# Turning the second branch's queries tile by tile between the products of the last projection

## The reference, cut to what matters

```python
def nsa_mixer(q, kv, gates, g_q, g_kc, g_ks, g_kw, pe_cmp, phi_k1, phi_k2, phi_v1, phi_v2):
    q = rms_norm(q.reshape(B, S, KH, G, dh), g_q)          # 8 heads of 64
    k_c, v_c, k_s, v_s, k_w, v_w = ...                     # six slices of kv, 2 heads each
    ...
    kc = rms_norm(compress(k_c, phi_k1, phi_k2), g_kc)     # compress: gelu(blocks @ w1) @ w2
    vc = compress(v_c, phi_v1, phi_v2)
    s_c = jnp.einsum('bsgqd,bcgd->bsgqc', q, kc)           # compressed branch
    ...                                                    # selected branch: q against k_s, v_s
    ...                                                    # window branch: q against k_w, v_w
    o = g[..., 0:1] * o_cmp + g[..., 1:2] * o_slc + g[..., 2:3] * o_win
```

## Time and profile before

| | us |
|---|---|
| median of 3 runs (761.27 to 831.82) | 761.53 |
| the profiled execution's own time | 763.1 |
| its span, first to last instruction | 761.4 |
| PE matmul busy | 752.5 |
| DVE busy | 420.0 |
| ACT busy | 368.8 |
| POOL busy | 137.7 |

### The profile page before, as it was taken

How to read it: one execution, slowest core, us unless ns; L and a number is a source line. 1 busy time by engine, 2 the same in 40 slices (tenths; PEclk the granted TensorE clock), 3 DMA queues, 4 the chain that set the end, 5 groups by cost and what they waited for, 6 DMA issues and landing times.

```text
span 761.4 us, 10546 instructions
## 1 busy us (share of the span) xinstructions
PE 752.5 (99%) x3869; PEld 629.5 (83%) x3869; DVE 420.0 (55%) x842; ACT 368.8 (48%) x719; POOL 137.7 (18%) x163
## 2 busy tenths in 40 slices
PE   9999989999999999999999999999999999999998
PEld 8998877877997788778888888888888888888886
DVE  5478779779986967648555333333334333333333
ACT  7768367756678887663343333333334232323230
POOL 3110336523556453300022000000000000000000
PEclk9999999999999999999999999999999999999999
DMA  9622121101111021113632332323232323232322
GB/s 339 230 79 66 56 74 67 55 28 56 56 56 56 28 84 36 48 56 89 216 91 85 103 111 84 110 84 111 83 111 84 110 84 111 83 111 84 110 84 110
DMA packets 21826, 70.82 MB, mean 93 GB/s; under 512 B 2448, under 2 KB 3600, under 8 KB 21520
## 3 DMA queue, kind: packets, MB, share of 16 engines
q1 hardware_dynamic: 21632, 70.13, 28.5%
q10 hardware_dynamic: 144, 0.03, 0.0%
HBM read 68.05 MB, written 2.10 MB: 92 GB/s over the span
## 4 chain that ended last, share of the span: by engine, by line
PE 93%; DVE 4%; POOL 1%; ACT 1%; issue 1%; POOLq 0%; DVEq 0%
PE psum L1535 26%; PE psum L1537 26%; PE psum L1536 26%; PE psum L1543 5%; PE psum L1718 4%; PE psum L1695 2%; PE psum L1696 2%; POOL nrstd L758 1%; DVE cmp_in L1262 1%; DVE x2T L1517 1%; PE psum L1550 1%; PE psum L1599 1%; ACT q_st L846 0%; PE psum L1690 0%; PE psum L1758 0%
## 5 line engine op out<-in xcount | busy, mean ns | idle before, releaser
L1133 DVE TENSOR_TENSOR w_lo<-stage,w_hi 128x1024 fp32r<-128x1024 f32 (+4 forms) x104 | 113.9, 1099 | 236.1 <-ACT w_hi L846 235.9
L846 ACT ACTIVATE w_hi<-stage 128x1024 fp32r<-128x1024 f32 (+4 forms) x150 | 125.5, 844 | 167.9 <-DMA stage<-in_panels 167.8
L1535 PE MATMUL psum<-hT_hi,w_hi 128*128 128x512 f32 x384 | 155.9, 406 | 0.0
L1537 PE MATMUL psum<-hT_hi,w_lo 128*128 128x512 f32 x384 | 150.1, 391 | 0.0
L1536 PE MATMUL psum<-hT_lo,w_hi 128*128 128x512 f32 x384 | 149.7, 390 | 0.0
L1535 PE MATMUL psum<-a_hi,w_hi 128*128 128x512 f32 x256 | 99.6, 389 | 0.0
L1536 PE MATMUL psum<-a_lo,w_hi 128*128 128x512 f32 x256 | 99.6, 389 | 0.0
L1537 PE MATMUL psum<-a_hi,w_lo 128*128 128x512 f32 x256 | 99.6, 389 | 0.0
L1537 PEld LDWEIGHTS psum<-hT_hi,w_lo 128*128 128x128 f32 x384 | 72.1, 188 | 15.3
L1536 PEld LDWEIGHTS psum<-hT_lo,w_hi 128*128 128x128 f32 x384 | 72.4, 189 | 12.6
L1535 PEld LDWEIGHTS psum<-hT_hi,w_hi 128*128 128x128 f32 x384 | 72.2, 188 | 12.5
(11 more groups left out here) (240 smaller groups left out, 1178.5 us busy)
## 6 DMA issues: line engine op xcount, KB each, us to landing
stage<-in_panels SPq DMA_DIRECT2D x104, 512.0 KB, 3.5
xT_in<-in_xT SPq DMA_DIRECT2D x8, 256.0 KB, 5.3
x_in<-in_x SPq DMA_DIRECT2D x4, 512.0 KB, 7.5
phi<-in_phi SPq DMA_DIRECT2D x2, 1024.0 KB, 6.2
x2T<-in_xT SPq DMA_DIRECT2D x1, 2048.0 KB, 9.9
out_xT<-x2T SPq DMA_DIRECT2D x8, 256.0 KB, 2.0
stage<-in_panels SPq DMA_DIRECT2D x8, 212.0 KB, 5.3
stage<-in_panels SPq DMA_DIRECT2D x4, 408.0 KB, 3.1
```

What stands on the lines that cost most here:

```text
L846: return nc.scalar.activation(dst, src, ACT.Copy, scale=scale)
L1133: tt_op(w_lo[:, p % SLOTS, cols], stage[:, p % SLOTS, cols], w_hi[:, p % SLOTS, cols].bitcast(F32), ALU.subtract)\
L1535: mm(dst, a_h, b_h, start=start, stop=False)
L1537: return mm(dst, a_l, b_h, start=False, stop=stop)
```

## The change

On PE all eight turns were in one place, after panel 1's products of the last projection, with panel 2's and the gelu's transpose put in between the second and the third tile, and panel 3's products after all of them. Now the order on PE is: turn tile 0, panel 2, turn tile 1, panel 3 of token tiles 0 and 1, `gelT`, turn tile 2, panel 3 of token tiles 2 and 3, turn tile 3. ACT rounds tile 0 before the Tanh, then panel 16, tile 1, two drains of the last projection, tile 2, two drains. DVE writes tile 0's low parts before it takes up the second half of the gelu. Of tile 3, ACT's roundings go into the `late` lists of units 0 and 1, DVE's low parts into the `early` lists of units 1 and 2. The banks of the last five uses become `gelT` in 4, (2,0) in 7, (2,1) in 6, (3,0) in 5, (3,1) in 4.

```diff
-    late = {1: [("kw_sq",)], 2: [("kw_sum",), ("kc",), ("gate_b",)], 3: [("kc_copy",), ("gate_fin",)], 4: [("kc_sq",)],
+    late = {0: [("qb_hi", 0)], 1: [("kw_sq",), ("qb_hi", 1)], 2: [("kw_sum",), ("kc",), ("gate_b",)], 3: [("kc_copy",), ("gate_fin",)], 4: [("kc_sq",)],
             5: [("kc_sum",)], 6: [("kwT",)], 9: [("kw_copy",)], 11: [("kcT",)]}
-    early = {4: [("kw_dup",)], 7: [("kw_low",), ("kc_dup",)], 12: [("kc_low",)]}
+    early = {1: [("qb_low", 0)], 2: [("qb_low", 1)], 4: [("kw_dup",)], 7: [("kw_low",), ("kc_dup",)], 12: [("kc_low",)]}
...
-    side += ["hidden"] + [("qbT", tt, half) for tt in range(2) for half in range(2)] + ["gelT"]
-    side += [("qbT", tt, half) for tt in range(2, TT) for half in range(2)]
+    side += ["hidden"] + [("qbT", tt, half) for tt in range(2) for half in range(2)]
...
+    for key, b in (("gelT", 4), (("qbT", 2, 0), 7), (("qbT", 2, 1), 6), (("qbT", 3, 0), 5), (("qbT", 3, 1), 4)):
+        bank.use(key, b)
...
             round_panel(15)
-            se.wait_ge(ev["gelu_in"], 1)
-            nc.scalar.activation(gel[:, :], gel[:, :], ACT.Tanh, scale=GELU_IN).then_inc(ev["tanh"], 1)
-            round_panel(16)
...
-            for tt in range(TT):
-                for half in range(2):
-                    round_q("qbT", tt, half, R_QB)
-            drain_proj(C_KV2, p_kv2)
+            round_qb(0)
+            se.wait_ge(ev["gelu_in"], 1)
+            nc.scalar.activation(gel[:, :], gel[:, :], ACT.Tanh, scale=GELU_IN).then_inc(ev["tanh"], 1)
+            round_panel(16)
+            round_qb(1)
+            drain_kv2(0)
+            drain_kv2(1)
+            round_qb(2)
+            drain_kv2(2)
+            drain_kv2(3)
...
+                elif kind == "qb_hi":
+                    round_q("qbT", TT - 1, a[0], R_QB)
...
             tt_op(gel[:, :], gel[:, :], hid[:, :], ALU.mult).then_inc(ev["gelu_in"], 1)
+            for half in range(2):
+                low_q("qbT", 0, half, R_QB)
             ve.wait_ge(ev["tanh"], 1)
...
-            for tt in range(TT):
+            for tt in range(1, TT - 1):
                 for half in range(2):
                     low_q("qbT", tt, half, R_QB)
...
+                elif kind == "qb_low":
+                    low_q("qbT", TT - 1, a[0], R_QB)
...
-            proj(C_KV2, 3)
+            turn_qb(0)
+            proj(C_KV2, 2)
+            turn_qb(1)
+            proj(C_KV2, 3, tts=range(0, 2))
+            te.wait_ge(ev["gelu"], 1)
+            transposes("gelT", [gel[:, :]])
+            turn_qb(2)
+            proj(C_KV2, 3, tts=range(2, TT))
+            turn_qb(3)
```

More of the change, by code:

```diff
@@ L1005, in round_q, with round_qb, drain_kv2 @@
                         .then_inc(high_done, 1)
-            for tt in range(TT):
+            def round_qb(tt):
                 for half in range(2):
                     round_q("qbT", tt, half, R_QB)
-            drain_proj(C_KV2, p_kv2)
+            def drain_kv2(tt):
+                drain_rows(("proj", C_KV2, tt), p_kv2[:, tt, :], PROJ[C_KV2][1], tt)
+            round_qb(0)
[8 more added lines that the diff above has]
+            drain_kv2(3)
             for kind, *a in script:
@@ L1277, in _ @@
             split_panel(15)
[L1279 to L1288, removed]
             def low_q(name, tt, half, gain):
@@ L1302, in low_q @@
                         ins.then_inc(even_low, 1)
-            for tt in range(TT):
+            ps = wait_full(ve, "hidden")
+            drained(nc.vector.tensor_copy(hid[:, :], ps[:, 0:HID]), "hidden")
+            wait_drained(ve, "hidden")
+            link(tt_op(gel[:, :], hid[:, :], hid[:, :], ALU.mult))
+            link(nc.vector.tensor_scalar(gel[:, :], gel[:, :], GELU_CUBE, 1.0, ALU.mult, ALU.add))
+            tt_op(gel[:, :], gel[:, :], hid[:, :], ALU.mult).then_inc(ev["gelu_in"], 1)
+            for half in range(2):
+                low_q("qbT", 0, half, R_QB)
+            ve.wait_ge(ev["tanh"], 1)
+            link(nc.vector.tensor_scalar(gel[:, :], gel[:, :], 1.0, 0.5, ALU.add, ALU.mult))
+            tt_op(gel[:, :], gel[:, :], hid[:, :], ALU.mult).then_inc(ev["gelu"], 1)
+            split_panel(16)
+            for tt in range(1, TT - 1):
                 for half in range(2):
@@ L1566, in first_k_tile, with proj @@
                     mm(dst[tt], hT_hi[:, 0, toks[tt]], w_lo[:, 0, 0:n], start=False, stop=False)
-            def proj(c, i, first_unit=None):
+            def proj(c, i, first_unit=None, tts=range(TT)):
                 p, n = 4 * c + i, PROJ[c][1]
@@ L1575, in proj @@
                 if i == 3:
-                    turns = [(kk, tt) for tt in range(TT) for kk in range(2)]
+                    turns = [(kk, tt) for tt in tts for kk in range(2)]
                 if p == 0:
@@ L1660, in _, with turn_qb @@
             proj(C_KV2, 1)
-            for tt in range(TT):
+            def turn_qb(tt):
                 te.wait_ge(qb_normed, tt + 1)
```

## The result

| | before | changed |
|---|---|---|
| median, us (16 runs each) | 761.63 | 763.21 |
| lowest, us | 761.27 | 762.47 |
| ratio of the runs, 95% interval | | 1.0018, 1.0011 to 1.0024 |
| profiled execution, us | 763.1 | 762.53 |
| its span, us | 761.4 | 760.8 |

The changed kernel is slower by 1.6 us, where I had forecast 0.1 less; 763.21 lies outside 758.9 to 762.9. One of the 16 runs of before took 831.82 us and is left out of the ratio. The profiled execution of the changed kernel is nevertheless the shorter one of the two, because its first turn comes 0.85 us earlier; behind that it is the longer one. The slower median goes back to TensorE's granted clock in single executions, which is what most of the experiments are about.

A forecast was written before the change was run, and what follows sets the result against it. PE was taken as the bound, with only its idle and slow time to win. -4.8 (earlier first score matmul) + 3.3 (wait at first probability transpose) + 1.4 (low clock) = -0.1 us, so 761.53 became 761.4; range 758.9 to 762.9.

The forecast's parts named there:

- the sum: Whole kernel: 4.8 us won, 3.3 lost to waiting and 1.4 to the clock, giving -0.1 us.
- my 4.8 us gain: First score matmul on PE at 99.9 instead of 104.73, 4.8 us earlier, the old slow clock stretch included.
- wait 1: PE at turn (2,1), bank 6, waits for DVE's low parts of (1,1): 0.9 us, range nothing to 1.75.
- wait 2: PE before the first probability transpose, bank 4, waits for DVE's second `qb_low`: 3.3 us, at least 1.8.
- low clock behind it: PE's clock halves around the wait before the first probability transpose, under filler products: 1.4 us, at most 1.7.
- everything behind the fifth score matmul: Later work keeps its old distances, shifted by 1.5 us, and was costed at nothing.
- B: Rival: clock stays up through the wait before the first probability transpose; -1.5 us, 760.0, down to 758.5; chance 0.27.
- C: Rival: hardly any wait before the first probability transpose, ACT reaching `qb_hi 1` sooner; -4.8 us, 756.7; chance 0.06.
- D: Rival: POOL stretches two moved low parts on DVE, units 1 and 2, by 0.71 us each; +1.4, 762.9; chance 0.12.
- E: Rival: wait at (2,1) near 1.75 us, clock falling around panel 3's first half instead; +0.8, 762.4; chance 0.05.

The follow-up runs named there:

- y0_after: The changed kernel, unchanged, timed again on another occasion beside the kernel before: 762.92 against 761.63 us, ratio 1.0019.
- by ring: The changed kernel with the two banks of the probability transposes taken in the other order, 5 then 4: 760.01 us, ratio to before 0.9973.
- by filler: The changed kernel with unit 3's five filler parts moved to unit 2, ahead of the first probability transpose: 760.38 us, ratio to before 0.9976.
- the ring and one top-k round in unit 0: The changed kernel with the probability transposes' banks swapped and unit 1's top-k round moved to unit 0: 760.22 us, ratio to before 0.9973.
- the halved wait: The changed kernel with both tile 3 roundings in unit 0 on ACT and both low parts in unit 1 on DVE: 760.29 us, ratio to before 0.9981.

## Why the prediction was wrong, point by point

The step that failed is the sum: "The profiled execution has a span of 761.4 and 763.1 in all; changed it would have 761.3 and 763.0. The median of the runs is 761.53, which I shift by the same amount". The profiled execution had a low stretch of the clock, 3.4 us long, and 1.5 us of my 4.8 us gain was that stretch. The kernel before has it in 59 of 104 executions, and its median lies between the two kinds. The typical pair is not always "fallen before, fallen after": in 45 of 104 executions it is "up before, fallen after". That the profiled execution stood 1.6 us above the median was in the table of times, and I carried a difference over without asking what that 1.6 us was. Most of it goes with the low stretch (the medians of the groups are 0.95 us apart); it was also dearer than most fallen ones, by 0.7 us against their median. My forecast for an execution like the profiled one, 763.0, lies close to the changed kernel's median of 763.2; carried over to a median that holds both kinds, it was wrong.

The second mis-sized term is the same clock behind the wait. I gave it at most 1.7 us. It measured 1.6 us in the profiles at 0.998 (the mean of 18 of the 30 executions) and 2.5 us in those at 0.996 (12 executions), where it falls inside the wait and lasts 6.8 us. From the first turn to the end: before 671.6 us (clock up) or 673.1 (fallen), changed 673.3 or 674.2 (761.5 less 87.25). Weighted by the counts (45 to 59, and 18 to 12) that is 672.5 and 673.7, 1.2 us apart. The mean times of all these executions are 1.1 us apart; the medians are 1.6 apart in the first result and 1.3 in y0_after. The agreement is in part luck, since the weights rest on one to three profiles of each kind and the time ahead of the first turn is left out.

The rest of the working held, like for like with the fallen execution. A wait is counted here as in the prediction, by how much later an instruction starts than it would without it; the idle time in the brackets of the timeline is up to 0.2 us shorter, because the matmul before counts as busy for longer than it holds up the next (0.38 against 0.19 us at (2,0)).

| term | predicted us | measured us |
|---|---|---|
| first turn to first score matmul | 11.6 | 11.52 |
| wait 1, at (2,1) | 0.9 | 0.8 |
| second `qb_hi` done, from the first score matmul | 5.40 | 5.54 |
| first probability transpose, from the same | 6.75 | 6.92 |
| wait 2 | 3.3 | 3.4 |
| low clock behind it | 1.4 | 1.61 (2.5 where it lasts 6.8) |
| everything behind the fifth score matmul | 0 | +0.1 |
| whole, against a fallen execution | -0.1 | +0.2 |

Wait 1 came as worked out: both of DVE's pauses were filled, it began the low parts of tile 1 at 94.02, 6.56 us after the first turn (forecast 6.59), and (2,1) started at 96.11 instead of 95.13 + 0.19 = 95.32.

The signs that I had named also came: the two waits in their places, no wait on `hid` or `ka`, full clock where the old low stretch was, no new wait behind unit 4. None of them looked at the step that failed. One slip of the prediction itself: its lower bound is given as B's long end at 758.9, while B is priced down to 758.5.

Of the rivals, B (the clock stays up) never happened in 30 executions. C is excluded by the wait itself. D's mechanism did not occur, as the earlier trace rows had said. The first moved pair of low parts, from 102.08 to 103.07, took 0.99 us beside POOL's pass; the second, from 104.75, took 1.00 with POOL idle.

```profile
101.61 1.28 POOL L823 TENSOR_TENSOR w_lo<-stage,w_hi 128x512 fp32r<-128x512 f32 x1 [14.94 <-ACT w_hi L848]
103.09 1.27 POOL L823 TENSOR_TENSOR w_lo<-stage,w_hi 128x512 fp32r<-128x512 f32 x1 [0.20 <-ACT w_hi L848]
```

The Trainium skill's page on GpSimd (GPSIMD Engine Reference, section 8, Key points) names contention only for a two-port mode or for two SBUF inputs, and the low parts read one tile from SBUF; the trace agrees.

E's second fall after the first half of panel 3 shows in no profile. The measured time is near D's 762.9, by another mechanism. None of the rivals was that the gain itself existed only in some executions, which is the one that I lacked.

What costs is shown to be the wait that the moves in the script make together with the bank order, not the moves by themselves: where the bank is free when PE comes, by ring or by filler, the new order with tile 3 still spread is 0.9973 and 0.9976 of the kernel before. These are the lowest ratios here, with the ring and one top-k round in unit 0 level with them; the interval of the halved wait (0.9981) overlaps theirs.

## What to carry to other kernels

When a step is moved behind others on two engines, follow the last use of each bank or buffer it holds to the next user, and count both queues up to it: here one entry in a ring decided 3.2 us of waiting. Before a difference is read off one profiled execution, set its time against the median of the runs; if it stands out, find what it has that the typical one lacks, and price the change against both kinds. An idle piece of PE costs its length and can cost a stretch at half clock with it, in all executions at 3.2 us here and, as far as is known, in some at 1.6 to 2.3 us; useful filler moved ahead of the wait took away both, while a later wait grew to 1.0 us.

## What was not expected of the hardware

The same program with the same waits keeps TensorE's clock in some executions and loses it in others: it stayed up in 45 and fell in 59 after 3.7 us with nothing but nine transposes, 7 and 4 with an idle piece of 1.6 us, 9 and 1 with one of 2.0 us, 3 and 7 with one of 2.3 us, 0 and 30 with one of 3.2 us. So the length of the idle piece alone does not rank them, though the counts are small. A low stretch lasted 3.4 us or 6.8 us. With gaps of 0.7, 0.5 and 0.7 us filled with products of 104 columns the clock stayed up in 10 of 10.

The fall also need not come while PE stands still: in the profiles at 0.998 it came 0.6 us after the products had begun again in the kernel before (99.22 against 98.63) and 0.95 to 1.3 us after in the three of the changed one (106.85 against 105.90 in the first). The clock records of the traces hint at what differs between executions. In the changed kernel the first turn stands 82.6 to 83.0 us behind the clock's first rise to full in the three profiles with a low stretch of 3.4 us, and 82.0 to 82.2 us behind it in the three with 6.8 us. In the kernel before it is 81.2 us in the two that fell and 80.9 in the one that stayed up. Within each kind the fall itself came at the same distance from that first rise, whatever the place of the code: 92.16 us in the two of before, 102.40 and 98.99 us in the three and three of the changed kernel. A few tenths of a us of the code against the clock's first rise may thus decide; no run set this distance on purpose, so it is not shown.
